# Loading the first two weight units as one pair, turning vectors with VectorE's block transpose, and fewer sums at the end of a two-layer decoder step

## The reference

```python
mod = (jax.nn.silu(c) @ w_ada + b_ada).reshape(B, N_MOD, D_MODEL)
s1, sc1, g1, s2, sc2, g2, s3, sc3, g3 = [mod[:, k] for k in range(N_MOD)]
h = modulate(x, s1, sc1)                      # x * (1 + scale) + shift
x = layer_norm(ALPHA * x + 0.5 * (1.0 + g1)[:, None] * swiglu(h, ffn1_wgu, ffn1_wdown), ln_g[0], ln_b[0])
h = modulate(x, s2, sc2)
proj = jnp.einsum('bld,de->ble', h, w_in)     # split into u_pool, u_lru, u_gate
...                                           # pool mixer, causal conv, gated recurrence (rglru)
x = layer_norm(ALPHA * x + (1.0 + g2)[:, None] * mix, ln_g[1], ln_b[1])
h = modulate(x, s3, sc3)
x = layer_norm(ALPHA * x + 0.5 * (1.0 + g3)[:, None] * swiglu(h, ffn2_wgu, ffn2_wdown), ln_g[2], ln_b[2])
```

## Time and profile before

| what | value |
|---|---|
| runs, us | 1016.41, 1016.82, 1016.4 |
| median, us | 1016.41 |
| the profiled execution, us | 1016.85 |
| its span, first to last instruction, us | 1014.7 |
| TensorE matmul busy | 999.8 us, 99% of the span |
| VectorE, ScalarE, GpSimd busy | 602.2, 458.2, 102.8 us |
| read from HBM | 233.11 MB, 231 GB/s over the span |

### The profile page before, as it was taken

The page is one execution under the profiler, slowest core; times in us unless marked ns, Lnnn a source line. Parts: engine busy times, 40 slices in busy tenths (PEclk is TensorE's granted clock), DMA queues, the critical chain, the costliest instruction groups (busy, mean ns, idle before and its releaser), DMA issues. The chain is left out here.

```text
span 1014.7 us, 19729 instructions
## 1 busy us (share of the span) xinstructions
PE 999.8 (99%) x8576; PEld 945.1 (93%) x8576; DVE 602.2 (59%) x908; ACT 458.2 (45%) x566; POOL 102.8 (10%) x160
## 2 busy tenths in 40 slices
PE   6999999999999999999999999999999999999997
PEld 4799999998988999999989999999998999999997
DVE  2356444556897755454567645455689866555563
ACT  3254443334685545343345434333468554444341
POOL 1060000000310430000005000000030034000000
PEclk9999999999999999999999999999999999999998
DMA  9998878876549797867677797858554867665631
GB/s 313 350 301 232 290 223 288 313 249 235 225 140 323 237 300 205 284 201 284 200 205 248 221 308 193 295 170 315 198 197 144 297 185 214 176 193 158 224 109 43
DMA packets 263159, 235.64 MB, mean 232 GB/s; under 512 B 7391, under 2 KB 240985, under 8 KB 263058
## 3 DMA queue, kind: packets, MB, share of 16 engines
q1 hardware_dynamic: 260960, 230.74, 72.0%
q0 software_dynamic: 2080, 3.58, 1.2%
q10 hardware_dynamic: 34, 0.07, 0.0%
HBM read 233.11 MB, written 1.78 MB: 231 GB/s over the span
## 5 line engine op out<-in xcount | busy, mean ns | idle before, releaser
L520 PE MATMUL bank<-m_hi,w_hi 128*128 128x264 f32 x1664 | 476.5, 286 | 0.4 <-DVE m_lo L1210 0.3
L521 PE MATMUL bank<-m_lo,w_hi 128*128 128x264 f32 x1664 | 471.9, 284 | 0.0
L522 PE MATMUL bank<-m_hi,w_lo 128*128 128x264 f32 x1664 | 471.3, 283 | 0.0
L1145 DVE TENSOR_TENSOR w_lo<-raw,w_hi 128x2048 fp32r<-128x2048 f32 (+3 forms) x154 | 334.0, 2169 | 211.6 <-ACT w_hi L898 210.8
L898 ACT ACTIVATE w_hi<-raw 128x2048 fp32r<-128x2048 f32 (+2 forms) x152 | 272.4, 1794 | 177.6 <-PE bank L522 159.2
L520 PEld LDWEIGHTS bank<-m_hi,w_hi 128*128 128x128 f32 x1664 | 313.4, 188 | 9.9 <-issue 8.0
L521 PEld LDWEIGHTS bank<-m_lo,w_hi 128*128 128x128 f32 x1664 | 313.6, 188 | 0.1
L522 PEld LDWEIGHTS bank<-m_hi,w_lo 128*128 128x128 f32 x1664 | 312.2, 188 | 0.0
L520 PE MATMUL bank<-h_hi,w_hi 128*128 128x264 f32 x672 | 193.6, 288 | 0.0
L522 PE MATMUL bank<-h_hi,w_lo 128*128 128x264 f32 x672 | 191.0, 284 | 0.0
L521 PE MATMUL bank<-h_lo,w_hi 128*128 128x264 f32 x672 | 190.7, 284 | 0.0
(11 more groups left out here) (233 smaller groups left out, 558.3 us busy)
## 6 DMA issues: line engine op xcount, KB each, us to landing
raw<-in_ffn_wgu_dram SPq DMA_DIRECT2D x168, 512.0 KB, 5.3
ada_raw<-in_w_ada_dram SPq DMA_DIRECT2D x72, 1024.0 KB, 9.3
raw<-in_ffn_wdown_dram SPq DMA_DIRECT2D x48, 512.0 KB, 3.6
raw<-in_ffn_wdown_dram SPq DMA_DIRECT2D x48, 384.0 KB, 4.4
raw<-in_w_in_dram SPq DMA_DIRECT2D x24, 512.0 KB, 4.6
raw<-in_w_out_dram SPq DMA_DIRECT2D x16, 384.0 KB, 6.1
raw<-in_w_out_dram SPq DMA_DIRECT2D x8, 256.0 KB, 7.0
x_rows<-in_x_prompt_dram SPq DMA_DIRECT2D x1, 1024.0 KB
```

The costliest lines, as they stand in the source:

```text
L520: pe.matmul(out, hi, r_hi, start=start, stop=False)
L521: pe.matmul(out, hi, r_lo, start=False, stop=False)
L522: mm = pe.matmul(out, lo, r_hi, start=False, stop=stop)
L1145: dve.tensor_tensor(w_lo[:, g % SLOTS, 0:n], raw[:, g % SLOTS, 0:n], w_hi[:, g % SLOTS, 0:n].bitcast(F32), ALU.subtract).then_inc(lo_split, 1)
```

## The change

Three things are changed.

1. **Units 0 and 1 are one pair.** Four DMAs of 512 KB load them in contiguous runs of 1 KB (256 columns): slot 0 then holds the gate tiles of both units, slot 1 the up tiles of both. `products` picks the tiles accordingly, and the split of unit 3 into slot 0 waits for unit 1 (`units_done` 2), as slot 0 is in use until then.
2. **Vectors are turned in square blocks.** The matmuls of a vector read their columns in an order with gaps (32 of every 128 columns), so that each 32x32 block of the result holds 32 neighbouring outputs. One VectorE transpose of 32x32 blocks, PSUM to SBUF, then replaces ScalarE's copy and TensorE's two matmuls. The slices do the same: 16 matmuls of 128 columns where 4 of 512 were, and no `slice_copy`, no `slice_sum`. The `keep_busy` counts change: 3 and then four times 5 where 6, 6, 6, 4, 2, 5 were, and 3 where 3 and 8 were.
3. **The end.** VectorE adds tile 6 to the running sums, so there are two groups of sums instead of three, all behind the last down unit. The second `turn_tiles` stands ahead of the sums of squares. The samples' sums are apart and come last, with their own deviation on ScalarE. VectorE takes the mean off three blocks before the variance instead of one. ScalarE stores `y_sample`.

```diff
+            def load_pair():
+                both = ffn1_wgu[0].rearrange("(e k p) (h d) -> h e p k d", e=2, p=P, h=2)
+                for h in range(2):
+                    dst = raw[:, h].rearrange("p (e k c) -> p e k c", e=2, c=2 * P)
+                    for e in range(2):
+                        sync.dma_start(dst[:, e], both[h, e, :, :, 0:2 * P]).then_inc(w_landed[h], 16)
...
-            load_unit(0)
-            load_unit(1)
+            load_pair()
...
                     for k in (2 * c, 2 * c + 1):
+                        columns = ada_raw[:, c, k % 2 * D:(k % 2 + 1) * D].rearrange("p (m g j) -> p g m j", g=4, j=32)
                         for g in range(4):
-                            first = k % 2 * D + g * QUARTER
-                            mm = pe.matmul(b[32 * g:32 * g + 32, 0:QUARTER], cT[:, k, :],
-                                           ada_raw[:, c, first:first + QUARTER], start=k == 0, stop=k == DT - 1,
+                            mm = pe.matmul(b[32 * g:32 * g + 32, 0:QUARTER].rearrange("p (m j) -> p m j", j=32),
+                                           cT[:, k, :], columns[:, g], start=k == 0, stop=k == DT - 1,
                                            tile_position=(0, 32 * g))
...
-                if g - 2 in FIRST_HALF:
-                    vector_turn(FIRST_HALF[g - 2])
...
                 for k in range(DT // HALVES):
-                    mm = pe.matmul(bank[6 + v][32 * k:32 * k + 32, :], cT[:, h * (DT // HALVES) + k, :],
-                                   ada_raw[:, i % ADA_SLOTS, k * SLICE:(k + 1) * SLICE],
-                                   start=h == 0, stop=h == HALVES - 1, tile_position=(0, 32 * k))
+                    columns = ada_raw[:, i % ADA_SLOTS, k * SLICE:(k + 1) * SLICE].rearrange("p (m g j) -> p g m j", g=4, j=32)
+                    for g in range(4):
+                        mm = pe.matmul(bank[6 + v][32 * g:32 * g + 32, 0:P].rearrange("p (m j) -> p m j", j=32),
...
-                    act.wait_ge(units_done, g - 2)
+                    act.wait_ge(units_done, 2 if g == SLOTS else g - 2)
...
-                dve.wait_ge(mod_out, a - 1)
-                turned = bank[6 + a % 2][:, QUARTER:QUARTER + DT * C].rearrange("p (h g c) -> p h g c", h=HALVES, c=C)
+                dve.wait_ge(ada_used, (a + 1) * CHUNKS)
+                dve.transpose(turned[:], bank[6 + a % 2][:, 0:QUARTER]).then_inc(vector_turned, 1)
+                dve.wait_ge(vector_turned, a - 1)
...
+                if (l, f) == (DEPTH - 1, 1):
+                    dve.wait_ge(evicted, n * DT + 7)
+                    dve.tensor_tensor(zsum[:], zsum[:], z[:, 6], ALU.add).then_inc(last_sum, 1)
+                    dve.wait_ge(squared, s + 4)
+                    dve.wait_ge(sums_ready, 2 * DEPTH)
+                    dve.tensor_tensor(sqs[:, 0], sqs[:, 0], sqs[:, 6], ALU.add).then_inc(last_sum, 1)
```

More of the change, by code:

```diff
@@ L169, in trunk @@
         rstd = sb("rstd", [P, T])
-        part = sb("part", [P, HALVES * P])
+        turned = sb("turned", [P, QUARTER])
         coef = sb("coef", [P, 2, DT, C])
@@ L554, in vector_whole @@
                 vector_half(a, 1)
[L556 to L565, removed]
             def beside(g):
@@ L626, in first_units @@
                 pe.wait_ge(init_read_act, DT // 2)
-                keep_busy(3, 6)
-                slice_part_of(0, 0, 0)
-                keep_busy(3, 6)
-                slice_part_of(0, 0, 1)
-                keep_busy(3, 6)
-                slice_part_of(0, 1, 0)
-                slice_sum(0, 0)
-                keep_busy(3, 4)
-                slice_part_of(0, 1, 1)
-                keep_busy(3, 2)
-                slice_sum(0, 1)
+                keep_busy(3, 3)
+                for v in range(2):
+                    for h in range(HALVES):
+                        slice_part_of(0, v, h)
+                        keep_busy(3, 5)
                 slice_part_of(1, 0, 0)
-                keep_busy(3, 5)
                 ready(pe, 1)
@@ L668, in up_phase @@
                         products(l, f, k)
-                if vector is not None:
-                    vector_turn(vector)
                 for n in range(2, UP_UNITS):
@@ L708, in down_phase @@
                         for i in range(2):
-                            if pair == 3 and third == 2 and i == 1:
+                            if pair == 3 and third == 2 and i == 1 and (l, f) != (DEPTH - 1, 1):
                                 pe.wait_ge(sums_ready, 2 * l + f + 1)
-                                if (l, f) == (DEPTH - 1, 1):
-                                    token_sums(MEAN, 6, 0, zsum[:])
-                                    token_sums(VAR, 7, 0, sqs[:, 0])
-                                else:
-                                    stat(bank[MEAN], mean_w, zsum[:], True, False)
-                                    stat(bank[VAR], mean_w, sqs[:, 0], True, False)
+                                stat(bank[MEAN], mean_w, zsum[:], True, False)
+                                stat(bank[VAR], mean_w, sqs[:, 0], True, False)
                             for k in range(7):
@@ L843, in mixer @@
                     ready(pe, g0 + i)
-                    if i == 1:
-                        vector_turn(gap)
                     if i == 2:
@@ L988, in up_phase @@
                         split(g + 2)
-                    beside(g - 1)
                     act.wait_ge(gate_done, turn + 1)
@@ L1030, in mixer @@
                 g0 = l * UNITS + IN
-                vector_copy(vector)
                 for i in range(IN_UNITS):
@@ L1077, in mixer @@
                 act.activation(rg[:], tt[:], ACT.Sqrt).then_inc(root_done, 1)
-                vector_copy(vector + 1)
                 split(g0 + 2)
@@ L1124, in _ @@
                    .then_inc(fin_copied, 1)
+            act.wait_ge(fin_copied, 2)
+            act.dma_start(y_sample.rearrange("b o d -> (b o) d"), ys_rows[:]).then_inc(y_stored, 16)
         @block.vector
@@ L1133, in _ @@
                .then_inc(init_read, 1)
-            own.did(dve.tensor_reduce(sum_w[:], ident[:].rearrange("p (g c) -> p c g", g=4), AX_X, ALU.add))
-            own.wait()
             for m in range(0, DT, 2):
```

151 lines of the change are left out of this document (65 added, 86 removed).

## The result

| kernel | median, us | runs, us | ratio to before, 95% interval |
|---|---|---|---|
| before | 1016.4 | 1015.99 to 1016.82 | |
| changed | 1011.1 | 1010.26 to 1011.87 | 0.9948 [0.9936, 0.996] |
| changed, once more in a later set | 1010.35 | 1009.86 to 1011.88 | 0.9942 [0.993, 0.9955] |

What follows compares the result with a forecast made beforehand. TensorE, busy 999.8 of 1014.7 us, was taken to bound the kernel, if its operands arrive in time. Start 4.3, vectors 4.3, mixers 0 and end 1.6 sum to 10.2, giving 1006.2 us, range 1003.3 to 1009.3.

Steps and rivals of the forecast that it cites:

- TensorE's side of the start: Start: first product at 29.5, fifth k tile at 40.4, so TensorE could be 6.6 us earlier at unit 2.
- it comes earlier only by what the bytes ahead cost less. That is the pair alone: Start, DMA: unit 5's data lands 2.3 us earlier, from the pair's faster transfer (7.7 to 5.4 us); start gains 4.3.
- the first rival: Unit 5 does not hold the start, which gains its full 6.6 to 7.8 us: 1003.9 to 1002.7; chance 0.12.
- A new wait of about 2.3 us: Ahead of unit 5, near 64 us: TensorE waits about 2.3 us for its data, while the start still gains 4.3.
- Vectors: Turns in or ahead of up and down units: 12 of 16 save TensorE 0.36 each, 4.3 us.
- its other estimate, 0.62: VectorE's 128x256 transpose at 0.62 us, from the skill's 311 ns for 128x128; the sum would be 0.3 us less.
- the mixers: Four turns, two per mixer: gain 0, with a gap of about 0.7 us ahead of each third `w_out` unit.
- End: After the last unit: 1.6 us gained, between 1.0 and 1.9, with the samples' store issued last at 1010.8.
- The fifth: Start: the clock stays at 1.2 GHz through the slices, about 5 us lost, 1011; chance 0.04.
- The second: Start: the pair is no faster, unit 5 gains only its 2.1 us of margin, 1008.4; chance 0.12.
- The third: All 16 vectors: reading with gaps slows their matmuls, 60.4 us in all; at 25% slower 1021.3; chance 0.07.

Runs made afterwards that it cites:

- e10: Kernel before with only the start of the change (pair, slices turned by VectorE), loads in old order: 1016.75 us, ratio 1.0007.
- e5: Kernel before with only the 16 later vectors turned by VectorE: 1010.92 us, ratio 0.9945.
- e6: Kernel before with only the end of the change: 1015.9 us, ratio 0.9992.
- e15: Kernel before with only the start of the change, and vector 2's 4 MB loaded behind units 7 and 8: 1010.01 us, ratio 0.9932.
- e1: Changed kernel with the pair undone, units 0 and 1 loaded one after the other in 512 B runs: 1011.97 us, ratio 0.9951.
- e3: Changed kernel with GpSimd's small row loads waiting for unit 4's split instead of unit 2's: 1009.16 us, ratio 0.9923.
- e4: Changed kernel with 18 idle-filling matmuls ahead of TensorE's wait for unit 5: 1008.74 us, ratio 0.9918.
- e12: Changed kernel with 18 idle-filling matmuls ahead of the wait for unit 5, run again beside the changed kernel: 1008.19 us, ratio 0.9919.
- e13: Changed kernel with VectorE's scaling waiting until GpSimd finished the samples' three operations: 1011.58 us, ratio 0.9945.
- e2: Changed kernel with vector 2's 4 MB loaded behind units 7 and 8 instead of behind unit 4: 1004.22 us, ratio 0.9875.
- e14: Kernel before with only vector 2's 4 MB moved behind units 7 and 8: 1016.87 us, ratio 1.0002.

## Why the prediction was wrong

The parts by themselves add up: start +0.35 (e10), vectors -5.75 (e5), end -0.77 (e6) make -6.2, where the whole measured -5.3 and -6.05. The forecast had -4.3, -4.3 and -1.6. Point by point:

- **TensorE's side of the start: right, and in part so close by luck.** First product 29.5 forecast, 29.36 found; fifth k tile 40.4 and 40.06; 6.6 us of lead forecast at unit 2, 7.0 found. The first slice took 1.87 us (17.46 to 19.33) and the later ones 1.01 (20.91 to 21.92), so that four make 4.9, about as much as four of the 1.24 that I kept (5.0). The chain from the first `keep_busy` to the end of the fourth slice took 10.65 where I had 10.22, and began 0.5 earlier in this trace (15.91 for 16.43). That TensorE's clock is the lower one at first is read from such doubled times of the same matmuls alone: the granted clock of that stretch is 1.00 in the earlier trace rows. e15 confirms the gain to the end, 6.6 us.
- **"it comes earlier only by what the bytes ahead cost less. That is the pair alone": the step that failed.** It failed twice. The pair was priced from a row that mixed run lengths, 391 GB/s, where its own came to 319; e1 values it at 0.75 us (0.35 to 1.2 over the traces), not 2.3. And the step took the queue ahead of unit 5 as fixed, though it has a second source: GpSimd's 21 loads wait on a split that the change itself made 6.5 us earlier. I named this only as a help ("out of its way") within the first rival; it was the opposite. e3 puts the weight of all these loads at 3.3 us of unit 5's landing; moving them forward cost 1.1 of it (e1 against before). Unit 5 landed 0.3 later than before instead of 2.3 earlier, and 1.55 and 1.1 are that difference.
- **"A new wait of about 2.3 us": its own price was left out.** A wait of TensorE was entered as lost lead and nothing more. It was 5.1 us, and the lower clock behind it took 1.7 to 2.7 more in the changed kernel's two traces. e4 and e12 give 2.2 to 3 back by filling it.
- **Vectors: mechanism right, term too small.** The 0.36 was right for what it measured, the distance to the next product, and missed the 0.08 that this product takes longer: 0.44. The transposes (442 ns for the 0.42 taken; by the forecast's own working its other estimate, 0.62, would have cost 0.2 in each mixer, 0.4 in all, where it says 0.3), the matmuls (381 ns, unchanged by the gaps) and the mixers (0.74 us of wait for 0.7, net nearly zero) came out as forecast.
- **End: 0.8 for 1.6.** The samples' store is last, as forecast. Its path was carried over from before at 4.45 us, though the change puts another VectorE operation beside GpSimd. The path took 5.43, and e13 measures the effect at 1.1 us.
- **The rivals.** None happened as written. The fifth named the number (1011) and the mechanism (a lower clock) but not the place: it fell behind the wait for unit 5, not among the slices. The first rival's world, the full lead, exists if vector 2's bytes stand elsewhere (e2, e15). The second was nearest in what it says of the pair. The third fell: 381 ns.

What stays open: the 0.7 MB of row loads would take 1.9 us at the 366 GB/s of their stage (an estimate); that all queues together went slower beside them (349 against 406 GB/s) goes with the rest of the 3.3, but was not taken apart. The two shares of the step that failed rest on one trace of e1, and between executions of the same code starts vary by up to 1.5 us and this landing by 0.8. And no run isolates why the slow stretch costs 1.7 us in one execution and 2.7 in another.

## What to carry to other kernels

When a change makes the critical engine faster, list every queue that is released by it: transfers that wait on its progress move forward too and may land ahead of the one load that has no slack. Price a new TensorE wait of several us at its length plus a slow stretch behind it, and before accepting it, look for bytes in the queue ahead that nobody needs yet: moving one line, worth nothing in the kernel before (e14), set 7 us free here, more than any part of the change gave alone. Read an instruction's cost from the distance between undisturbed neighbours on both sides, not to the next start alone.

## What the runs showed of the hardware that I had not expected

- With a wait of 5.1 us up to 68.73, TensorE's granted clock was 0.50 from 69 to 72 us and 0.84 from 72 to 80; 36 records of idle-filling work in the wait kept it at 1.00.
- GpSimd's operation on 128 x 64 elements took 0.31 us beside an idle VectorE or one reading an operand from PSUM, and 0.76 beside one with both operands in SBUF. VectorE's operation there was hardly touched (2.82 against 2.74 for four).
- 21 row loads, 0.7 MB in all, ahead of a 1 MB load made it land 3.3 us later (e3), though they were not new: 0.4 MB of them stood ahead of it in the kernel before too.
- Runs of 1 KB instead of 512 B in the first two units raised the rate of 5.5 to 12.5 us from 273 to 319 GB/s.
- A float32 matmul that reads 32 of every 128 columns takes as long as one that reads them in a row, 381 ns.
- A product behind two 36-column matmuls holds TensorE for 0.21 us instead of 0.12, at all 16 turns of the kernel before.
